# Value blocks start with the tiles whose banks are free, and a query block is served inside the context parts

## What is computed

```python
def even_project(u, w_in, ...):            # layer 0, context and latent tokens
    z = (u @ w_in).astype(jnp.float32)     # 21 feature blocks and 8 half value blocks
    gq, gk, gv, gg, ga, mq, mk, mv, mo, mg = jnp.split(z, splits, axis=-1)
    gq, gk = apply_rope(gq, *rope_gla), apply_rope(gk, *rope_gla)
    log_a = jax.nn.log_sigmoid(a_pre) / GLA_TAU
...
def gla_chunked(q, k, v, log_a, state0):
    b = jnp.cumsum(log_a, axis=3)          # the running sums of the decays
    q_dec = q * jnp.exp(b)
    k_dec = k * jnp.exp(-b)
...
def na_mixer(u_lat, u_ctx, w_qkv, w_out, rpb, need_ctx):   # layer 1
    q, k, v = heads(u_lat @ w_qkv, T, 3)
    kc, vc = heads(u_ctx @ w_qkv[:, D:], n_ctx, 2)
```

## Time and profile before

| | us |
|---|---|
| median of the timed runs | 1807.78 (1807.19 to 1808.2) |
| the profiled execution, its own time | 1804.66 |
| its span, first to last instruction | 1802.7 |
| PE busy in the span | 1733.4 (96%) |

### The profile page before, as it was taken

The page is one execution under the profiler, slowest core; times in us unless marked ns, Lnnn a source line. Parts: engine busy times, 40 slices in busy tenths (PEclk is TensorE's granted clock), DMA queues, the critical chain, the costliest instruction groups (busy, mean ns, idle before and its releaser), DMA issues. The chain is left out here.

```text
span 1802.7 us, 26300 instructions
## 1 busy us (share of the span) xinstructions
PE 1733.4 (96%) x9650; PEld 1492.8 (83%) x9650; DVE 898.9 (50%) x1420; ACT 751.6 (42%) x1182; POOL 543.4 (30%) x249
## 2 busy tenths in 40 slices
PE   6999999997999999999999999999999999999999
PEld 2677788996899999999988887987567788888877
DVE  4778876667956666666424242000774522222344
ACT  3572444775433223233333343212784433334442
POOL 0222123553222332332232223322002344444442
PEclk9999999998999999999999999999999999999999
DMA  8323223343334334334212212112321232322221
GB/s 331 136 71 133 80 94 106 126 122 130 128 117 140 120 114 140 117 118 140 71 60 65 64 47 82 61 58 69 116 85 48 64 100 93 102 97 94 94 94 59
DMA packets 66585, 184.05 MB, mean 102 GB/s; under 512 B 5920, under 2 KB 26784, under 8 KB 65200
## 3 DMA queue, kind: packets, MB, share of 16 engines
q1 hardware_dynamic: 44784, 164.69, 26.8%
q10 hardware_dynamic: 21696, 17.88, 3.3%
HBM read 180.40 MB, written 2.15 MB: 101 GB/s over the span
## 5 line engine op out<-in xcount | busy, mean ns | idle before, releaser
L636 POOL TENSOR_TENSOR wsp<-raw,wsp 128x1024 fp32r<-128x1024 f32 x201 | 495.7, 2466 | 1198.6 <-ACT wsp L701 1197.9
L701 ACT ACTIVATE wsp<-raw 128x1024 fp32r<-128x1024 f32 x201 | 213.6, 1063 | 492.5 <-PE ps L2055 387.7
L2055 PE MATMUL ps<-u,wsp 128*128 128x512 f32 (+1 forms) x1560 | 404.1, 385 | 3.5 <-ACT naq L1202 2.7
L2055 PEld LDWEIGHTS ps<-u,wsp 128*128 128x128 f32 x1560 | 293.7, 188 | 60.0 <-ACT naq L1202 3.1
L2054 PE MATMUL ps<-v_a,wsp 128*128 128x384 f32 x1008 | 341.4, 339 | 0.0
L2055 PE MATMUL ps<-v_b,wsp 128*128 128x386 f32 x1008 | 340.8, 338 | 0.0
L2435 PE MATMUL ps<-hsp,wsp 128*128 128x512 f32 x1056 | 302.4, 391 | 2.5 <-DVE hsp L1789 2.5
L2435 PEld LDWEIGHTS ps<-hsp,wsp 128*128 128x128 f32 x1056 | 196.7, 187 | 46.8 <-issue 4.3
L2055 PEld LDWEIGHTS ps<-v_b,wsp 128*128 128x128 f32 x1008 | 190.5, 189 | 0.0
L2054 PEld LDWEIGHTS ps<-v_a,wsp 128*128 128x128 f32 x1008 | 189.2, 188 | 0.0
L1806 DVE SCALAR_TENSOR_TENSOR conv<-apad,vec,conv 128x770 f32<-128x770 f32 (+1 forms) x44 | 47.1, 1069 | 215.5 <-ACT conv L1112 215.5
(11 more groups left out here) (277 smaller groups left out, 2274.6 us busy)
## 6 DMA issues: line engine op xcount, KB each, us to landing
raw<-in_weights SPq DMA_DIRECT2D x281, 512.0 KB, 3.8
nab<-in_nabias ACTq DMA_DIRECT2D x32, 256.0 KB, 2.7
start_w<-in_start SPq DMA_DIRECT2D x6, 1024.0 KB, 20.5
h<-in_x SPq DMA_DIRECT2D x4, 768.0 KB, 14.0
mD<-rows_scratch ACTq DMA_DIRECT2D x12, 256.0 KB, 4.1
mqs<-rows_scratch ACTq DMA_DIRECT2D x12, 256.0 KB, 5.1
h<-in_x ACTq DMA_DIRECT2D x2, 1536.0 KB, 6.5
start_w<-in_start SPq DMA_DIRECT2D x4, 512.0 KB, 12.2
```

The costliest lines, as they stand in the source:

```text
L636: pool.tensor_tensor(wsp[:, s % 2, 1, :], raw[:, raw_index(s) % 4, :], wsp[:, s % 2, 0, :].bitcast(F32), ALU.subtract).then_inc(*own.one(l ...
L701: act.activation(wsp[:, s % 2, 0, :], raw[:, raw_s % 4, :], ACT.Copy).then_inc(*own.one(hi_ready))
L2055: mm = pe.matmul(lat, w, x_lat[:, k, xp, :], start=first, stop=last)
```

## The change

Three edits. In layer 0 the first value round takes its tiles for `k == 0` in the order 1, 3, 4, 5, 2, 0, and each waits only for what was in its own bank: tile 1 for feature block 3, tiles 3 to 5 for the gate rows, tile 2 for the context part of block 4, tile 0 for block 4. In layer 1 the order is 0, 2, 3, 4, 5, 1, and all but tile 1 wait for query and key block 14 only. In layer 1 `context_high` is cut into four parts behind `qk(1)` and four behind `qk(2)`.

```diff
-            def context_high(q, B):
+            def context_high(q, B, ks):
...
-                for k in range(KT):
+                for k in ks:
...
             for n in range(N_QK):
                 qk(n, 0, 0)
                 if n == 1:
-                    context_high(norm[2], shift(1, 0))
+                    context_high(norm[2], shift(1, 0), range(4))
+                if n == 2:
+                    context_high(norm[2], shift(1, 0), range(4, KT))
...
-            def tokens(s, b, taken, done):
+            def tokens(s, b, taken, done, order):
...
-                    for i in range(TILES):
+                    for i in order if k == 0 else range(TILES):
...
-                first = lambda i: [(in_act_took, N_FIRST), (in_dve_took, N_FIRST - 1), (rows_taken, 4), (cx_took, N_FIRST)]
+                first = lambda i: [[(in_act_took, N_FIRST), (in_dve_took, N_FIRST - 1)],
+                                   [(in_act_took, N_FIRST - 1), (in_dve_took, N_FIRST - 2)],
+                                   [(cx_took, N_FIRST)]][i] if i <= 2 else [(rows_taken, 4)]
...
-                    tokens(S_V + 4 * cg + b, b, again if cg else first, v_done)
+                    tokens(S_V + 4 * cg + b, b, again if cg else first, v_done, range(TILES) if cg else (1, 3, 4, 5, 2, 0))
...
-                first = lambda i: [(qk_taken, N_QK)]
+                first = lambda i: [(qk_taken, N_QK if i == 1 else N_QK - 1)]
...
-                    tokens(S_V1 + 4 * cg + b, b, again if cg else first, nav_done)
+                    tokens(S_V1 + 4 * cg + b, b, again if cg else first, nav_done, range(TILES) if cg else (0, 2, 3, 4, 5, 1))
```

## The result

| | before | after |
|---|---|---|
| median of five runs each, taken side by side | 1807.78 (1807.19 to 1808.91) | 1799.06 (1796.37 to 1799.81) |
| ratio | | 0.9933 (0.9909 to 0.9956) |
| profiled execution, its span | 1804.66, 1802.7 | 1798.48, 1796.6 |

The changed kernel is faster. The two medians are 8.7 us apart. The ratio is not their quotient, which would be 0.9952; it makes 12.1 us of 1807.78 (8.0 to 16.5), and I forecast 8.3.

What follows compares the result with a forecast made beforehand. PE, busy 1733.4 of 1802.7 us, was taken as the bound, so time could be won only where it waits or works slowly. Terms 4.41 + 3.92 + 0 = 8.33 us; 1807.78 - 8.33 = 1799.45 us, range 1796 to 1803.

Steps and rivals of the forecast that it cites:

- Value round of layer 1: Layer 1, first value round: the new tile order removes PE's 2.23 us wait and 1.69 us of slow clock, gain 3.92 us.
- Query block 4: Layer 1, before query block 4: splitting the context parts removes a 2.70 us stall and 1.71 us of slow clock, 4.41 us.
- Rival (b): Layer 1: the stall at query block 4 comes back at block 5, costing 3.7 us, 1803.1 us; chance 0.08.
- Layer 0 inside one execution: Layer 0 value rounds: PE waits 0.3 us, then 4.8 us before block 2, loses 3.0 us to clock, passes 147.99 as before.
- Layer 0 as a term of the sum: Layer 0, first value round: the new tile order removes the 3.91 us wait but gains 0 us in total.
- PE cannot pass 147.99 earlier, however early it is: Layer 0, second value round, tile 1: PE waits for DVE's copy of bank 1, whose list never waits for PE.
- My bounds: Layer 0 gain: a loss of 2.8 us if the clock stays low twice as long, at most 6.6 us gained.
- Rival (a): Layer 0: this edit pays too, needing DVE's list to end earlier; up to 6.6 us more, 1792.8 us; chance 0.06.
- Rival (c): Waits go but slow clock stretches turn up elsewhere: 1.7 us for one, 3.4 for both, 1802.9 us; chance 0.12.
- (d): Layer 0: after the longer pause the clock stays low to the end of the value blocks, slower, 1818.5 us; chance 0.02.
- (e): The edits don't do what they say, because awaited counts fall together with something later; no size given; chance 0.02.
- The base: Whole kernel before the change: median of timed runs 1807.78 us, from which the forecast gain of 8.33 us was subtracted.

## Why the prediction was right or wrong

- **Value round of layer 1**, forecast 3.92: right on the wait. No wait, clock 1.00, 4.1 us in the pair of traces; the timing of the edit alone (-2.5, interval from -6.2 to +1.1) allows it. The 1.69 us for the clock are less certain: in three of eleven profiles with that wait no slow stretch follows it.
- **Query block 4**, forecast 4.41: right in place and size. 4.6 us in the pair, -5.4 (2.4 to 8.3) in the timing. The low part of block 4 was done 1.8 us before block 3 ended (I had 1.7).
- **Rival (b), block 5**: didn't happen, and by the margin that was worked out. Its high part ran at 1103.56, the low part ended at 1104.70 + 2.39 = 1107.1, and block 4 lasted until 1102.8 + 5.6 = 1108.4: 1.3 us in hand, where I had 1.2. The hold-up of the fifth low part came as 1.44 us (1099.87).
- **Layer 0 inside one execution**: right step by step. PE waits 0.40 us before tile 0 (0.3), 4.69 us before block 2 (4.8), loses 2.9 us to the clock (3.0), and passes the second round's tile 1 at 42.2 us behind feature block 4, where it was 42.3.
- **Layer 0 as a term of the sum**, "the gain is 0": wrong; the measurement says 4.5 us (2.2 to 6.9). The failed step is the cost of the old order, which I read from one execution: "PE cannot pass 147.99 earlier, however early it is" holds in every trace, but it isn't the whole cost. When the first slow stretch is short, the old order turns the time won into a longer pause, 2.6 us instead of 1.4, and that pause goes with executions that are 4.3 us longer by the end of layer 0, though two of these four lose most of it in a low stretch elsewhere. In the new order PE arrives together with the copy and there is no pause. My bounds took the length of the slow stretch as uncertain for the new order only, never for the old. In the means of the timed runs 1.8 us of it are lower clock and 2.5 are not, and the cause of these 2.5 stays open.
- **Rival (a)** held, then, by another mechanism than the one named: DVE's list ended at most 0.3 us earlier. Its price, 6.6 us, was near the upper end of the interval.
- **Rival (c)** happened in part. The slow stretches behind the two waits of layer 1 went, one ahead of the query blocks became longer (0.66 against 0.89 over 15 us), and over the timed runs the two layer 1 edits save 0.5 us of lower clock where I had 3.4. In the pair of traces it doesn't show in the sum, because others became shorter; the timing of the two edits together (4.3 to 10.7 us) is too wide to tell.
- **Rivals (d), (e)**: neither. The clock was back within 7 us behind the 4.69 us. The same 4.7 us stand in the profiles of the layer 0 edit alone, which is faster than before.
- **The base.** I took 1807.78 from runs that agreed within a microsecond as the level of the kernel before. Its runs went from 1801.7 to 1821.4 us in later sessions, and the execution with the profile, 1804.66, was among the shortest. A cost that appears only in the longer ones is invisible in such a profile.

What is shown: that the missing gain comes with the layer 0 edit (with this edit alone, and by taking it out of the change), that the wait at the second round varies between executions, that a change in DVE's list which leaves the 3.9 us ahead of the first round and removes the later wait gains as much, and that a PE that is 1.2 to 5.2 us late lets POOL's difference in ahead of DVE's product, which adds 3.9 us and more. What is only argued: that the wait at the second round is what the layer 0 edit removes to its profit. The profiles account for 2.2 us up to B, and part of that is lower clock in places that the edit doesn't touch.

## What to carry to other kernels

A wait whose length depends on something that varies between executions, such as how long the clock stays low, has to be priced over several profiled executions; profile the kernel before at least three times, and once in a long one. If PE is early at a fixed point, time won before it is worth nothing in the waits, but taking the pause away may still pay. A low stretch of the clock that goes in one place can come back in another, so a forecast should count it apart from the wait, and the granted clock of the timed runs says what became of it. Measure idle matmuls in the trace before a reading rests on their length. And look at which of two instructions that can't overlap comes first: here a delay of 1.2 us decided it and cost 5.6 us in the trace.

## What the runs showed of the hardware

- The same 3.9 us of idle time, with the same instructions behind it, was followed by the lower clock level for 6.0 of the next 8.4 us in some executions (mean clock 0.64) and for 3.2 in others (0.81).
- A pause of 1.4 us had full clock behind it in each of five executions. One of 2.6 us had full clock behind it in three, and 1.2 GHz for 6.8 us in one (0.50 over 6.8 us). In layer 1 one of 2.2 us had the lower level behind it in eight profiles (0.74 over 6.5 us in the first) and full clock in three (1.00 over 6.5 us). So the length of the pause alone doesn't decide.
- Executions of one kernel, unchanged, took from 1801.7 to 1821.4 us. In its five profiled ones most of the difference is the granted clock: 0.985 in the one of 1804.66 us and 0.979 in the one of 1814.37 us.
- A product of 128x1024 on DVE takes 1.22 us, and 3.39 us when POOL's difference of 128x1024 has begun 0.6 us before it (187.09 and 187.66); then it ends 1.1 us behind POOL's. By the Trainium skill, SBUF — State Buffer, section "Who interferes with whom", a DVE instruction with two SBUF inputs and a GpSimd instruction that reads SBUF exclude each other and the later one waits in full. The traces agree: POOL's own part goes from 2.40 to 2.69 us where DVE's product was first and overlapped its start.
